# Attention probabilities transposed by VectorE in 32x32 blocks, head outputs and sums of squares from small TensorE tiles

## The reference, cut to what matters

```python
xn = _rmsnorm(x, norm_g)
q, k, v, b_gate, c_gate, h, g_attn, g_conv = jnp.split(xn @ w_in, SPLITS, axis=-1)
q = _rope(_rmsnorm(q.reshape(b, t, N_HEADS, HEAD_DIM), q_norm_g), pos)
...
sc = jnp.einsum('bqkgd,bskd->bkgqs', qg, kc).astype(jnp.float32) * SCALE
m = jnp.maximum(jnp.max(s, axis=-1, keepdims=True), sink)
p = jnp.exp(s - m)
probs = p / (jnp.sum(p, axis=-1, keepdims=True) + jnp.exp(sink - m))
attn = jnp.einsum('bkgqs,bskd->bqkgd', probs.astype(vc.dtype), vc)
...
merged = sigmoid(g_attn) * (attn @ w_attn_proj) + sigmoid(g_conv) * (z @ w_conv_proj)
x = x + merged @ w_out
x = x + (silu(xn @ w_ffn_gate) * (xn @ w_ffn_up)) @ w_ffn_down
```

## Time and profile before

| | |
|---|---|
| median of three runs | 1737.02 us |
| the profiled execution's own time | 1736.81 us |
| its span (first to last instruction) | 1735.0 us |
| TensorE products: busy, count | 1715.4 us (99%), 13944 |
| TensorE weight loads: busy, count | 1700.1 us (98%), 13944 |
| VectorE busy | 1014.1 us (58%) |
| ScalarE busy | 808.6 us (47%) |
| GpSimd busy | 30.9 us (2%) |
| mean granted TensorE clock | 0.996 of full |

### The profile page before, as it was taken

One profiled execution on the slowest core, in us unless ns is written; L12 is line 12 of the kernel. 1 busy time (PEld: TensorE's weight loads), 2 busy tenths in 40 slices (PEclk: granted clock), 3 DMA queues, 4 the chain that ended last, 5 costly groups with the idle time before them and its releaser, 6 DMA issues.

```text
span 1735.0 us, 35645 instructions
## 1 busy us (share of the span) xinstructions
PE 1715.4 (99%) x13944; PEld 1700.1 (98%) x13944; DVE 1014.1 (58%) x1267; ACT 808.6 (47%) x983; POOL 30.9 (2%) x53
## 2 busy tenths in 40 slices
PE   8899999999999999999999999999999999999999
PEld 7899999999999999999999999999999999999999
DVE  6876776767754444555466555554555554455565
ACT  5455556456554454443444555543343443334443
POOL 0100000000000000000000000000000000000000
PEclk9899999999999999999999999999999999999999
DMA  7455545554575555555565555565556556556554
GB/s 239 142 154 163 157 145 164 163 157 145 155 226 179 174 179 181 174 177 182 171 194 181 170 181 175 170 189 180 178 173 183 178 173 188 176 175 186 174 175 154
DMA packets 298466, 302.73 MB, mean 174 GB/s; under 512 B 9456, under 2 KB 296304, under 8 KB 298304
## 3 DMA queue, kind: packets, MB, share of 16 engines
q1 hardware_dynamic: 296384, 296.00, 56.0%
q10 hardware_dynamic: 1440, 3.14, 0.6%
q0 software_dynamic: 608, 3.11, 0.5%
HBM read 299.50 MB, written 2.72 MB: 174 GB/s over the span
## 4 chain that ended last, share of the span: by engine, by line
PE 76%; issue 22%; DVE 1%; DMA 0%; ACT 0%; POOL 0%; DVEq 0%; ACTq 0%; POOLq 0%
PE acc L969 24%; PE acc L970 24%; PE acc L971 24%; PE side L1045 1%; DMA region_x<-in_x_t 0%; PE side L1069 0%; PE side L1057 0%; PE side L1033 0%; DVE w_lo L571 0%; PE side L1047 0%; DVE region_m L622 0%; PE side L1059 0%; PE side L1072 0%; DVE region_m L630 0%; PE side L1076 0%
## 5 line engine op out<-in xcount | busy, mean ns | idle before, releaser
L571 DVE TENSOR_TENSOR w_lo<-raw,w_hi 128x1024 fp32r<-128x1024 f32 x568 | 690.0, 1225 | 540.1 <-ACT w_hi L367 531.8
L367 ACT ACTIVATE w_hi<-raw 128x1024 fp32r<-128x1024 f32 x568 | 594.2, 1054 | 612.4 <-PE acc L971 608.9
L969 PE MATMUL acc<-xn_hi,w_hi 128*128 128x288 f32 x3008 | 865.5, 288 | 5.5 <-DVE w_lo L571 5.4
L970 PE MATMUL acc<-xn_lo,w_hi 128*128 128x288 f32 x3008 | 862.0, 287 | 0.0
L971 PE MATMUL acc<-xn_hi,w_lo 128*128 128x288 f32 x3008 | 861.9, 287 | 0.0
L969 PEld LDWEIGHTS acc<-xn_hi,w_hi 128*128 128x128 f32 x3008 | 570.0, 189 | 7.7 <-DVE w_lo L571 4.2
L970 PEld LDWEIGHTS acc<-xn_lo,w_hi 128*128 128x128 f32 x3008 | 570.1, 190 | 0.1
L971 PEld LDWEIGHTS acc<-xn_hi,w_lo 128*128 128x128 f32 x3008 | 570.0, 189 | 0.0
L969 PE MATMUL acc<-at_hi,w_hi 128*128 128x288 f32 x1216 | 347.9, 286 | 0.5 <-DVE w_lo L571 0.5
L971 PE MATMUL acc<-at_hi,w_lo 128*128 128x288 f32 x1216 | 347.9, 286 | 0.0
L970 PE MATMUL acc<-at_lo,w_hi 128*128 128x288 f32 x1216 | 347.9, 286 | 0.0
(11 more groups left out here) (169 smaller groups left out, 724.1 us busy)
## 6 DMA issues: line engine op xcount, KB each, us to landing
raw<-in_w_in SPq DMA_DIRECT2D x200, 512.0 KB, 4.4
raw<-in_w_ffn_gate SPq DMA_DIRECT2D x88, 512.0 KB, 4.3
raw<-in_w_ffn_up SPq DMA_DIRECT2D x88, 512.0 KB, 4.5
raw<-in_w_ffn_down SPq DMA_DIRECT2D x64, 512.0 KB, 3.7
raw<-in_w_attn_proj SPq DMA_DIRECT2D x32, 512.0 KB, 4.4
raw<-in_w_conv_proj SPq DMA_DIRECT2D x32, 512.0 KB, 4.3
raw<-in_w_out SPq DMA_DIRECT2D x32, 512.0 KB, 4.5
raw<-in_w_ffn_down SPq DMA_DIRECT2D x32, 384.0 KB, 3.6
```

The lines of the kernel that those rows point to most:

```text
L367: nc.scalar.activation(w_hi[:, s], raw[:, s], ACT.Copy).then_inc(S["hi_ready"], 1)
L571: V.tensor_tensor(w_lo[:, s], raw[:, s], w_hi[:, s].bitcast(F32), ALU.subtract).then_inc(S["lo_ready"], 1)
L969: te.matmul(out, w_hi[:, s, k, cols], hi_b, start=first, stop=False)
L970: te.matmul(out, w_hi[:, s, k, cols], lo_b, start=False, stop=False)
```

## The change

Probabilities are no longer transposed by TensorE into the accumulators and copied out by ScalarE. VectorE transposes them from memory to memory in blocks of 32x32, right after it has normalised them. A block of 32 keys therefore lies on each quarter of the partitions, and `heads_out` multiplies quarter by quarter: stationary tiles of 32 rows (keys) by 64 columns (values), in eight positions of the array. GpSimd lays out the values once per key head so that each quarter has all 13 blocks of 32 keys (`stage_values`, 20 copies). The sums of squares are made with stationary tiles of 64 rows by 64 columns, as are the scores of the sample frames, whose queries need no zeroed halves now. `heads_out` moves to the place after piece 0 of group `g + 3`; TensorE's stream is interrupted twice a round rather than three times. ScalarE's and VectorE's steps for the output move ahead of those for the convolution's output. TensorE's loop now holds two rounds, and rounds 0 and 1 are written out.

```diff
+            def stage_values(head):
+                for q in range(4):
+                    at = slice(QUARTER * q, QUARTER * q + QUARTER)
+                    for r in range(4):
+                        own.mark(nc.gpsimd.tensor_copy(
+                            blocks[at, :, r], values_all[QUARTER * r:QUARTER * r + QUARTER, head, 0:3, :]))
+                    own.mark(nc.gpsimd.tensor_copy(values_cur[at, KEY_BLOCKS - 1], values_all[0:QUARTER, head, 3, :]))
...
-                act.wait_ge(S["probs_in_psum"], j + 1)
-                nc.scalar.activation(probs_t_first.rearrange("p h n -> p (h n)"),
-                                     side[:, 0:2, :].rearrange("p b n -> p (b n)"), ACT.Copy)
-                nc.scalar.activation(probs_t_second[:], side[:, 2, :], ACT.Copy)
-                nc.scalar.activation(probs_t_sample[:, 0], side[:, 3, 0:P], ACT.Copy)
-                nc.scalar.activation(probs_t_sample[0:TS, 1], side[0:TS, 3, P:2 * P], ACT.Copy
-                                     ).then_inc(S["probs_copied"], 1)
...
+                for half in range(2):
+                    r = slice(64 * half, 64 * half + 64)
+                    own.mark(V.tensor_scalar(probs_sample[r], probs_sample[r], of_sample(s_inv, half), None, ALU.mult))
+                own.settle()
+
+                V.transpose(probs_t[:].rearrange("p u k -> p (u k)"), probs.rearrange("p u k -> p (u k)"))
+                V.transpose(probs_t_sample, probs_sample).then_inc(S["probs_turned"], 1)
                 ahead(g + 3, 1)
                 ahead(g + 3, 2)
...
             def head_sums(j):
-                pe.wait_ge(S["q_squared"], j + 2)
-                each_head = same_head.rearrange("p (h c) -> p h c", h=2)[:, :, 0]
+                wait_apart(pe, S["q_squared"], j + 2)
                 for n in range(2):
                     for t in range(2):
-                        c = 4 * n + 2 * t
-                        te.matmul(head_ssq[:, c:c + 2], head_b[:, t, n * HALF:n * HALF + P], each_head, start=True,
-                                  stop=True)
-                te.matmul(head_ssq[:, 8:9], squares_sample[:].rearrange("p h t n -> p (h t n)"), ones[:, 0:1],
-                          start=True, stop=True)
+                        for part in halves:
+                            for half, r in enumerate(halves):
+                                at = n * HALF + part.start
+                                te.matmul(head_ssq[part, half, 2 * n + t:2 * n + t + 1], head_b[r, t, at:at + 64],
+                                          ones[r, 0:1], start=True, stop=True)
+                for part in halves:
+                    for half, r in enumerate(halves):
+                        te.matmul(head_ssq[part, half, 4:5], squares_sample[r].rearrange("p t n -> p (t n)"),
+                                  ones[r, 0:1], start=True, stop=True)
...
+            def heads_out(j, head):
+                pe.wait_ge(S["values_staged"], head + 1)
+                pe.wait_ge(S["probs_turned"], j + 1)
+                quarters = [slice(QUARTER * q, QUARTER * q + QUARTER) for q in range(4)]
+                of_heads = probs_t[:].rearrange("p (t r) (m k) -> p r t m k", t=2, m=3)
+                blocks = TP // QUARTER
+                for kb in range(blocks):
+                    for q, rows in enumerate(quarters):
+                        for half, r in enumerate(halves):
+                            at = (kb % 4) * QUARTER
+                            if kb < 4:
+                                te.matmul(side[r, q, 0:P], values_cur[rows, kb],
+                                          of_heads[rows, half, :, 0:2, at:at + QUARTER], start=kb == 0, stop=False)
+                            else:
+                                te.matmul(side[r, q, 0:P].rearrange("p (t m n) -> p t m n", t=2, m=2)[:, :, 1],
+                                          values_cur[rows, kb], of_heads[rows, half, :, 2, at:at + QUARTER], start=False,
+                                          stop=kb == blocks - 1)
+                for kb in range(blocks, KEY_BLOCKS):
+                    for q, rows in enumerate(quarters):
+                        at = (kb - blocks) * QUARTER
+                        last = te.matmul(side[halves[q // 2], q, P:P + TS], values_cur[rows, kb],
+                                         probs_t_sample[rows, at:at + QUARTER], start=kb == blocks,
+                                         stop=kb == KEY_BLOCKS - 1)
                 last.then_inc(S["out_t_in_psum"], 1)
...
                 for s in range(SLOTS):
                     piece(g + 3, s, 2, xn_hi, xn_lo)
-                    if s == 1:
-                        transpose_probs(j)
-                heads_out(j)
-
-            mix(0, first=True)
-            with pe.Fori(1, PAIRS) as j:
-                mix(j)
+                    if s == 0:
+                        heads_out(j, head)
+
+            mix(0, 0, first=True)
+            mix(1, 0)
+            with pe.Fori(1, KV_HEADS) as head:
+                mix(2 * head, head)
+                mix(2 * head + 1, head)
```

More of the change, by code:

```diff
@@ L202, in encoder_layer, with of_sample @@
         state_cur = sb("state_cur", [P, 2, 2])
[L203 removed]
+        stats = sb("stats", [P, 9, ROWS])
         s_max, s_neg, s_sink, s_sum, s_inv, s_rms, s_scale, row_rms, row_ms = (
[L206 removed]
+            stats[:, n] for n in range(9))
+        def of_sample(column, half):
+            return column[64 * half:64 * half + 64, 5 * half + 4:5 * half + 5]
         in_rms = sb("in_rms", [P, T])
@@ L419, in _ @@
                 nc.scalar.activation(prompt(head_b), sums(0, slice(0, TP)), ACT.Square)
[L420 to L423, removed]
+                nc.scalar.activation(split(squares_sample), sums(0, slice(TP, T)), ACT.Square).then_inc(S["q_squared"], 1)
                 ahead(g + 2, 0)
@@ L670, in _ @@
             last.then_inc(S["values_ready"], 1)
+            own.mark(V.memset(stats[:, 0:5], 0.0))
             dve.wait_ge(S["rows_in_psum"], 1)
-            own.mark(V.tensor_copy(row_rms[:, 0:8].rearrange("p (n u) -> p n u", n=2),
-                                   wide(side[:, 3, 0:2].rearrange("p (n o) -> p n o", o=1), P, 2, 4)))
-            own.mark(V.tensor_copy(row_rms[:, 8:9], side[:, 3, 2:3]))
+            for half in range(2):
+                own.mark(V.tensor_copy(row_rms[:, 5 * half:5 * half + 4].rearrange("p (n t) -> p n t", n=2),
+                                       wide(side[:, 3, 0:2].rearrange("p (n o) -> p n o", o=1), P, 2, 2)))
+                own.mark(V.tensor_copy(row_rms[:, 5 * half + 4:5 * half + 5], side[:, 3, 2:3]))
             own.settle()
@@ L706, in _ @@
                 own.settle()
[L707 to L710, removed]
+                V.tensor_copy(split(q_sample), sample(head_a)).then_inc(S["q_roped"], 1)
                 dve.wait_ge(S["q_squared"], j + 2)
@@ L724, in _ @@
                             scalar=lowest, op0=ALU.add, op1=ALU.max, accum_out=s_max[:, c:c + 1]))
-                own.mark(V.reduce_max(s_max[:, 8:9], scores_sample, AX_X))
+                for half in range(2):
+                    own.mark(V.reduce_max(of_sample(s_max, half), scores_sample(half), AX_X))
                 dve.wait_ge(S["head_rms_ready"], j + 1)
@@ L787, in _ @@
                 ahead(g + 4, 1)
+                dve.wait_ge(S["attn_hi_ready"], j + 1)
+                for t in range(2):
+                    V.tensor_tensor(by_quarter(at_lo_p[:, j, t]), out_t[:, t], by_quarter(at_hi_p[:, j, t].bitcast(F32)),
+                                    ALU.subtract)
+                for half in range(2):
+                    r = slice(64 * half, 64 * half + 64)
+                    last = V.tensor_tensor(sample(at_lo_p[r, j]), split(out_sample_t[r, half]),
+                                           sample(at_hi_p[r, j].bitcast(F32)), ALU.subtract)
+                last.then_inc(S["side_free"], 1)
                 ahead(g + 4, 2)
@@ L1064, in heads_out @@
-            def heads_out(j):
-                pe.wait_ge(S["probs_copied"], j + 1)
-                rows = [slice(64 * half, 64 * half + 64) for half in range(2)]
-                for half, r in enumerate(rows):
-                    te.matmul(side[r, 0, :], values_cur[:, 0], probs_t_first[:, half], start=True, stop=False)
-                for half, r in enumerate(rows):
-                    second = probs_t_second[:, 2 * half * P:2 * (half + 1) * P].rearrange("p (t n) -> p t n", t=2)
-                    te.matmul(out_t[r, :, P:2 * P], values_cur[:, 1], second, start=False, stop=True)
-                for half, r in enumerate(rows):
-                    te.matmul(side[r, 1, 0:2 * TS], values_cur[:, 2], probs_t_sample[:, 0, r], start=True, stop=False)
-                for half, r in enumerate(rows):
-                    last = te.matmul(side[r, 1, 0:2 * TS], values_cur[0:TS, 3], probs_t_sample[0:TS, 1, r], start=False,
-                                     stop=True)
+                for half, r in enumerate(halves):
```

(8 more changed lines are left out.)

111 lines of the change are left out of this document (52 added, 59 removed).

## The result

| | before | after |
|---|---|---|
| median (lowest to highest), five runs each | 1737.02 us (1736.59 to 1738.07) | 1747.83 us (1744.14 to 1752.45) |
| ratio, 95% interval | | 1.0064 (1.005 to 1.0077) |
| profiled execution, its span | 1736.81, 1735.0 us | 1752.45, 1750.7 us |
| mean granted TensorE clock | 0.996 | 0.989 |

The change makes the kernel 0.6% slower. The forecast had the sign right and the size wrong: +57 us, measured +10.8.

The account below looks back on a forecast made before the run. TensorE's interrupted stream was taken to bound the kernel. Per round, +6.35 us for heads_out and +0.8 for the first interruption, 7.15 over eight rounds, added 57.2 to 1736.8: 1794 us, own range 1772 to 1820.

Parts of the forecast that it names:

- TensorE's stream bounds the kernel: Mixer round before the change: 384 products take 47.04 us, three interruptions the other 6.5 of 53.57 us.
- A pass costs the sequencer 0.0625 us: TensorE's small tiles: load and product are two sequencer steps of 0.031 us; own range 0.050 to 0.080 us.
- the term of +6.35 us for `heads_out`: Each round: 168 passes, 16 of them queued, take 9.9 us in place of 3.55 for transposes and outputs.
- The queue of 16: Passes estimated to wait queued when an interruption starts, between 2 and 28; each worth 0.5 us in all.
- the first interruption +0.8: Sums and scores in each round: 3.8 us against 2.99, with 1.5 us for the 40 passes of head_sums.
- The scores' 1.5 us: Scores in the first interruption keep their present 1.5 us, passes arriving as fast as the tiles want them.
- a slack of 0.7: VectorE's transposes end at 147.6, heads_out starts at 148.33, so they cost nothing; at half pace 10 us in all.
- rival 4: VectorE or GpSimd late: +10 us and more under Rival 1, giving 1735 us; chance 0.03.
- The longer loop body: TensorE's two-round loop: the jump costs 0; three jumps at the longest sequencer wait, 2.67 us, would be 8 us.
- Rival 1: Small tiles set the pace, sequencer keeps up: heads_out 2.16 us against 3.55, 1725 us in all; chance 0.14.
- below about 0.022 us per pass: Pace of handing over small tiles below which Rival 1 decides and the forecast would be wrong in sign.
- Rival 3: As forecast, and TensorE's clock falls during thin array use in heads_out: 14 to 27 us more, 1808 to 1821; chance 0.11.

Follow-up runs that it names:

- e3: The kernel before the change with only TensorE's loop holding two rounds, rounds 0 and 1 written out: 1748.06 us, ratio 1.0062 to the kernel before.
- e1: The changed kernel with TensorE's loop holding one round and the values announced once a round: 1730.02 us, ratio 0.9957 to the kernel before.
- e8: e1 with 26 small float32 products (104 instructions) put in ahead of round 0 on TensorE: 1727.26 us, ratio 0.9948 to the kernel before.
- e5: e1 with the products of heads_out made twice, 336 passes a round: 1756.64 us, ratio 1.0116 to the kernel before.
- e9: e1 with 64 small float32 products (256 instructions, a whole packet) put in ahead of round 0: 1729.49 us, ratio 0.9958 to the kernel before.
- e6: e1 with 104 semaphore increments put in on TensorE ahead of round 0: 1734.99 us, ratio 0.999 to the kernel before.

## Why the prediction was right in sign and wrong in size

1. *TensorE's stream bounds the kernel; a round is 47.04 us and its interruptions.* Right. 47.04 + 2.82 + 2.57 = 52.43 us is the undisturbed round measured.
2. *A pass costs the sequencer 0.0625 us.* This is the step that failed, and with it the term of +6.35 us for `heads_out`. Measured: -0.98 us. The forecast took the 0.03 us between a first load and its product behind a held sequencer as the pace of handing over. The stopped `heads_out` is the direct counterproof. Behind an empty queue, the view of 99.85:100.0 us has

```profile
99.91 0.31 PE L1112 MATMUL side<-region_m 32*64 32x32 f32 x8 [1.32 <-issue]
99.91 0.20 PEld L1112 LDWEIGHTS side<-region_m 32*64 32x64 f32 x8 [1.46 <-issue]
```

   eight loads and eight products started within 0.1 us, and 40 passes took 100.62 - 99.91 = 0.71 us. So 0.03 us is a delay of a first pair and not a rate; what makes it the runs don't show. The queue of 16 that the forecast allowed matters little at this price. The page of the Trainium skill that the prediction weighed, "TensorE: Matmul & The Clock Gate" (section "Wait — 56ns, not 53.3ns?"), gives about 62 ns per MATMUL with hardware decode off and about 25 ns at least; 0.0129 us for a load with its product lies below both, and the measurement decides.
3. *`head_sums` 1.5 us, the first interruption +0.8.* Wrong for the same reason: 0.69 us and -0.17. The scores' 1.5 us was right (239.07 - 237.56).
4. *VectorE's transposes 1.84 and 0.3 us, a slack of 0.7.* Right. VectorE in order of time, beside the earlier trace rows:

```profile
256.91 0.62 DVE L780 TENSOR_SCALAR region_x<-region_x,stats 64x160 f32<-64x160 f32 x2
257.57 1.78 DVE L783 STREAM_TRANSPOSE probs_t<-region_x 128x1536 f32<-128x1536 f32 x1
259.27 0.30 DVE L784 STREAM_TRANSPOSE region_m<-region_x 128x160 f32<-128x160 f32 x1
259.50 2.32 DVE L594 TENSOR_TENSOR w_lo<-raw,w_hi 128x1024 fp32r<-128x1024 f32 x2
```

   They end at 259.57 and `heads_out` starts at 260.26. GpSimd's copies and ScalarE cost nothing either, as forecast: no wait for them stands in any round, and rival 4 did not happen.
5. *The longer loop body: "I take 0".* The second failed step, and the one that makes the kernel slower. The prediction named the number of jumps (three, really two that go back) and a bound of 8 us, but priced the jump and not the code behind it. Two jumps stop TensorE for 6.9 us, and e3 shows 11.5 us in all for the loop edit alone. The body of 2 x 1224 instructions is 157 KB at 64 bytes, so `heads_out` is fetched in every round too: five stops, 7.4 us. In e1 only the two rounds that are fetched anyway pay.
6. *Rival 1, the tiles set the pace: 1725 us.* It was nearly right in size (`heads_out` 2.57 us against its 2.16) and had been given 0.14. With the instructions in the right place its time is almost reached as well: 1727.26 in e8, and 8 x 0.41 = 3.3 us of `heads_out` are what it set too low. That the tiles set the pace is borne out for the passes of 128 columns: they start 0.015 us apart, those of 64 columns 0.011 (58 from 261.21 to 261.85), though each is one load and one product. What holds back the shorter ones no run shows. The forecast let this rival decide "below about 0.022 us per pass"; that is where the sign turns, while its 1.81 us over 152 passes would set the pace only from 0.012 down.
7. *Rival 3, the clock falls.* The clock did fall, but not through thin use of the array in `heads_out`: three rounds show 1.00, each with a stopped `heads_out` in it. It fell behind the stops of 3.5 us and in two other rounds with a stop in `heads_out`, and cost 7.9 us. That is a remainder; the count of products behind round 4's stop bears out its share.

The forecast thus held two errors of opposite sign. For passes and sums it took 8 x 7.15 = +57 us where 8 x -1.14 = -9 us was measured, 66 us too much. For the fetching it took nothing where 7.4 + 6.9 + 7.9 = 22 us were measured in that execution. Only the second makes the kernel slower, so the sign was right for a wrong reason.

The Trainium skill, "Runtime: NRT & Kernel Launch" (section "Instruction fetch mechanics"), says that instructions are refilled in blocks of 16 KiB, 256 instructions, and that a taken branch whose target is not in the current window of two pages waits for a fetch. The runs agree on the packets of 16 KB and on the wait, 3.1 to 4.5 us at such a jump. They do not agree on the window: the bodies of e1 (78 KB) and e5 (100 KB) are jumped back over without a stop, and the measurement decides. The page also calls crossing a block mostly hidden; that holds for the main stream in every kernel here, and not for `heads_out`, whose 336 instructions take 2.4 us.

Open: how much code is held. 100 KB stayed (e5), 113 KB did not (e3), and nothing between was run. That a packet is fetched at each stop is seen, but at which instruction a packet ends was shifted (e8, e9) and not located, so which rounds of after stop could not have been told ahead. Why the clock fell behind some stops of 1.5 us and not behind others stays open.

## What to carry to other kernels

Count the instructions of a loop body on the engine that sets the end, at 64 bytes each, whenever an edit unrolls a loop or splits a product into many small ones: a body that was held and no longer is costs several microseconds at every jump, and more for the clock behind it. A dense run of small tiles is cheap (0.013 us per load and product) only from code that is held already, and where it must be fetched its place in the 16 KB packets is worth trying. A delay seen once at the head of a queue is not a rate: before pricing 150 instructions by it, look for a run that has at least as many, or keep the cheap end as the forecast's equal. A stop for which the profile names no releaser is best laid beside the packets of instructions: here every one ended shortly behind such a packet.

## What the runs showed of the hardware

- A float32 pass on 32x64 tiles, load and product, costs 0.0129 us on average in `heads_out`: 168 more passes (64 of 128 columns, 64 of 64, 40 of 32 for the sample frames) in 2.16 us (e5).
- In all 29 stops of over 0.8 us in the mixer, in the eight traces that have any, TensorE goes on 1.3 to 1.9 us after the end of a 16 KB packet of instructions.
- A block of 128x1536 float32 is transposed in 32x32 blocks by VectorE in 1.78 us, the pace of its ordinary float32 work in the earlier trace rows.
- 104 semaphore increments on TensorE's queue outlast a wait of 7.0 us by 6.7 us (e6), so they are far dearer than 26 products in the same place, during which TensorE still waited 5.2 us (e8).
